# Second mixer of a hybrid decode trunk: the norm of k moved out of k and into the gates' exponent, k·k first in a head

## The reference

```python
conv = silu(causal_conv4(proj[..., :GDN_QKV]))
q = l2_normalize(conv[..., :HK]) * GDN_DK ** -0.5
k = l2_normalize(conv[..., HK:2 * HK])          # k * rsqrt(sum(k*k) + 1e-6)
v = conv[..., 2 * HK:]
g = -exp(a_log) * softplus(a + dt_bias)
beta = sigmoid(b)
# in chunks of C tokens: Gc = cumsum(g)
decay = exp(where(incl, Gc[i] - Gc[j], -inf))
M = eye(C) + where(strict, beta[i] * (k k^T) * decay, 0)
W = M^-1 (beta * exp(Gc) * k) ; U = M^-1 (beta * v)
# over the chunks: u = U - W S ; o = q_dec S + (q k^T * decay) u ; S = g_last * S + k_dec^T u
o = rms_norm(o, o_norm) * silu(z) ; y = o @ w_out
```

## Time and profile before

| what | us |
|---|---|
| median of 3 runs (lowest to highest) | 1335.26 (1334.72 to 1336.23) |
| the profiled execution, device time | 1334.86 |
| its span, first to last instruction | 1332.9 |
| TensorE busy | 1309.3 (98%) |
| VectorE / ScalarE / GpSimd busy | 634.4 / 507.1 / 365.9 |
| granted TensorE clock, mean over the span | 0.998 of full speed |

### The profile page before, as it was taken

The page is one execution under the profiler, slowest core; times in us unless marked ns, Lnnn a source line. Parts: engine busy times, 40 slices in busy tenths (PEclk is TensorE's granted clock), DMA queues, the critical chain, the costliest instruction groups (busy, mean ns, idle before and its releaser), DMA issues.

```text
span 1332.9 us, 28024 instructions
## 1 busy us (share of the span) xinstructions
PE 1309.3 (98%) x11596; PEld 1086.3 (81%) x11596; DVE 634.4 (48%) x1009; ACT 507.1 (38%) x785; POOL 365.9 (27%) x506
## 2 busy tenths in 40 slices
PE   8999999999999999999999999999999999999997
PEld 7766588888888888887778777877888888888886
DVE  5447653333333322267776677766633333332222
ACT  6243453222222322244555465545432223222221
POOL 1004324121212100165453545453221222211010
PEclk9999999999999999999999999999999999999999
DMA  8658422422232232111212221122223222233211
GB/s 264 209 191 278 143 96 95 149 102 99 94 122 104 101 121 85 63 64 40 89 41 88 88 72 57 73 96 66 96 105 116 94 94 94 94 118 131 88 44 64
DMA packets 32140, 140.89 MB, mean 106 GB/s; under 512 B 4634, under 2 KB 6938, under 8 KB 20155
## 3 DMA queue, kind: packets, MB, share of 16 engines
q1 hardware_dynamic: 32058, 139.75, 30.2%
HBM read 128.63 MB, written 11.11 MB: 105 GB/s over the span
## 4 chain that ended last, share of the span: by engine, by line
PE 92%; DVE 4%; ACT 1%; issue 1%; DMA 1%; SPq 0%; DVEq 0%; ACTq 0%
PE P L1745 64%; PE P L2110 10%; PE P L2303 2%; DVE wl L1486 1%; PE P L2288 1%; PE P L2365 1%; PE P L2296 1%; PE P L2119 1%; PE P L1823 1%; PE P L2125 1%; PE P L2331 1%; PE P L2345 1%; PE P L1955 1%; PE P L2321 1%; PE P L1898 1%
## 5 line engine op out<-in xcount | busy, mean ns | idle before, releaser
L1745 PE MATMUL P<-zh,wh 128*128 128x260 f16 x1712 | 329.2, 273 | 2.1 <-DVE wl L1194 2.1
L1745 PE MATMUL P<-zl,wh 128*128 128x260 f16 x1712 | 329.0, 273 | 0.0
L1745 PE MATMUL P<-zh,wl 128*128 128x260 f16 x1712 | 329.0, 273 | 0.0
L1174 DVE SCALAR_TENSOR_TENSOR wl<-stage,wh 128x2048 f16<-128x2048 f32 (+1 forms) x75 | 185.3, 2471 | 195.4 <-ACT wh L761 192.8
L1745 PE MATMUL P<-arena,wh 128*128 128x260 f16 x1816 | 276.2, 273 | 1.0 <-DVE hT L1391 0.3
L1745 PEld LDWEIGHTS P<-arena,wh 128*128 128x128 f16 x1816 | 175.0, 97 | 29.2 <-issue 1.3
L1745 PEld LDWEIGHTS P<-zh,wh 128*128 128x128 f16 x1712 | 164.3, 97 | 34.0 <-issue 6.7
L1745 PEld LDWEIGHTS P<-zh,wl 128*128 128x128 f16 x1712 | 165.6, 97 | 25.9
L1745 PEld LDWEIGHTS P<-zl,wh 128*128 128x128 f16 x1712 | 165.4, 97 | 25.8
L1745 PE MATMUL P<-arena,wl 128*128 128x260 f16 x908 | 174.5, 273 | 0.0
L761 ACT ACTIVATE wh<-stage 128x2048 f16<-128x2048 f32 (+1 forms) x80 | 161.8, 2023 | 3.6 <-PE P L1745 3.6
(11 more groups left out here) (366 smaller groups left out, 1646.3 us busy)
## 6 DMA issues: line engine op xcount, KB each, us to landing
stage<-w_gu SPq DMA_DIRECT2D x44, 1024.0 KB, 4.8
stage<-w_in SPq DMA_DIRECT2D x23, 1024.0 KB, 4.9
stage<-w_dn SPq DMA_DIRECT2D x16, 1408.0 KB, 5.8
arena<-cache_k SPq DMA_DIRECT2D x32, 256.0 KB, 3.5
stage<-w_out SPq DMA_DIRECT2D x8, 1024.0 KB, 5.4
arena<-cache_v SPq DMA_DIRECT2D x32, 256.0 KB, 3.0
arena<-delta_state SPq DMA_DIRECT2D x8, 512.0 KB, 3.5
o_ds<-arena SPq DMA_DIRECT2D x8, 512.0 KB, 6.8
```

The source lines that it names most:

```text
L1174: nc.vector.scalar_tensor_tensor(out=wl[:, j, 0:words], in0=stage[:, j, 0:words], scalar=WS, in1=wh[:, j, 0:words], op0=MUL, op1=SUB).then ...
L1745: mm = nc.tensor.matmul(pm[j][:, c, :], w[:, wslot, o:o + 128], x[:, k, c * CH:(c + 1) * CH], start=(k == first and w is wh and x is xh), ...
```

## The change

k stays unnormalised. With n_i = |k_i| and r_i = 1/n_i the triangular system is written in other variables (each row and column scaled by a power of the token's norm), so that beta and 1/|k|² come in as logarithms added to the exponent from which `et` is formed, and v is scaled by |k| (`kn`) instead of by beta. |k|² is the diagonal of the raw k·k.

- TensorE: k·k is the first step of a head, on raw k, and no longer needs `kb`. The 512-column broadcast of beta is gone, and `stat_l2` with it (in its place behind chunk 2 stands a `fill(1)`, taken from chunk 0, whose `fill(3)` is now `fill(2)`). The 8-column matmul over `qkp` is a 16-column one over `qkk`, moved to the head's start as the last of `gb_ps`. `k·q` waits for `rk` as well as `gd` and `bd`.
- VectorE: four `tensor_tensor_reduce` of k·k with the identity (`dg`, each two instructions) come first in a head, then `add_query` of the last head (which stood at that head's end), then `tj` (4 columns, both inputs in SBUF), then `ex` as before, `bd` as a product, no `kb`. `decode_update` has one more small step. Ahead of head 0 there are three more operations of 520 columns on 8 partitions, and beta's row is formed here.
- ScalarE: `norm_l2` is gone. Five small operations come in ahead of `et`, and `gam` moves from before `ex` to behind `yi`, ahead of the split.
- GpSimd: `square_k` and `normalize_k` are gone; `decode_products` (four small operations) moves into the previous head; `kbg` moves ahead of `om`.

The diff, cut to what the prediction speaks of (`...` marks what is left out):

```diff
@@ gpsimd, loop over the heads
-                pool.wait_ge(nq, h + 1)
-                if h >= 1:
-                    pool.wait_ge(kqs_ps, h)
-                nc.gpsimd.tensor_copy(kd2, two(k[:, SEQ:]))
...
                 pool.wait_ge(*G("gd", h + 1))
                 pool.wait_ge(st_in[h % 2], 16 * (h // 2 + 1))
...
                 nc.gpsimd.tensor_tensor(v, v, gD[:, h, :].unsqueeze(2).to_broadcast([128, NDEC, 128]), MUL
                                         ).then_inc(sdec, 1)
+                pool.wait_ge(*G("gam", h + 1))
+                if h >= 1:
+                    pool.wait_ge(*G("ws_ps", 3 * h))
+                nc.gpsimd.tensor_tensor(kbg_w, k[:, 0:SEQ], gamB, MUL).then_inc(S["kbg"], 1)
                 pool.wait_ge(*G("nf", h + 1))
...
-                pool.wait_ge(*G("gam", h + 1))
-                pool.wait_ge(*G("kk_ps", h + 1))
-                nc.gpsimd.tensor_tensor(kbg_w, kbg_w, gamB, MUL).then_inc(S["kbg"], 1)
...
-                    square_k(p)
+                    decode_products(p)
                     square_q(p)
                     decode_conv(p, (2,))
-                    normalize_k(p)
@@ scalar, loop over the heads
                 act.wait_ge(*G("gb_ps", h + 1))
-                nc.scalar.activation(gamB, P[:, 2, :], ACT.Exp).then_inc(S["gam"], 1)
                 nc.scalar.activation(gD[:, h, :], P[:, 7, 0:8], ACT.Exp).then_inc(S["gd"], 1)
+                nc.scalar.activation(rk, P[:, 7, 24:32], ACT.Ln, bias=epsc[:, 2:3]).then_inc(S["lr"], 1)
+                act.wait_ge(*G("dg", h + 1))
+                nc.scalar.activation(klog, ksq, ACT.Ln, bias=epsc[:, 2:3]).then_inc(S["lk"], 1)
+                act.wait_ge(*G("lr", h + 1))
+                nc.scalar.activation(rk, rk, ACT.Exp, scale=-0.5)
+                nc.scalar.activation(qks, P[:, 7, 16:24], ACT.Copy).then_inc(S["rk"], 1)
+                act.wait_ge(*G("lk", h + 1))
+                nc.scalar.activation(kn, klog, ACT.Exp, scale=0.5).then_inc(S["kn"], 1)
                 act.wait_ge(*G("ex", h + 1))
...
+                nc.scalar.activation(gamB, P[:, 2, :], ACT.Exp).then_inc(S["gam"], 1)
                 next_split("in1", h, 1)
...
-                                                       ACT.Copy, scale=tokm[:, c, 32 + h:33 + h])
+                                                       ACT.Copy, scale=kn[:, c:c + 1])
...
-                    if c == 2 and p < HG:
-                        norm_l2(p)
@@ vector, loop over the heads
-                dve.wait_ge(*G("gd", h + 1))
-
+                dve.wait_ge(*G("kk_ps", h + 1))
+                for c in range(4):
+                    ins = nc.vector.tensor_tensor_reduce(out=dg_out[c], in0=P[:, 6, c * 128:(c + 1) * 128], in1=ident[:, :],
+                                                         scale=1.0, scalar=0.0, op0=MUL, op1=ADD,
+                                                         accum_out=ksq[:, c:c + 1])
+                ins.then_inc(S["dg"], 1)
+                if n >= 0:
+                    add_query(n)
+                dve.wait_ge(*G("lk", h + 1))
+                link(nc.vector.tensor_tensor(tj, tokg[:, :, h], klog, ADD))
                 for c in range(4):
...
-                                                   scalar=tokm[:, c, h:h + 1], in1=msk[:, 1, :], op0=SUB, op1=MIN)
+                                                   scalar=tj[:, c:c + 1], in1=msk[:, 1, :], op0=SUB, op1=ADD)
...
-                dve.wait_ge(nq, h + 1)
-                nc.vector.tensor_tensor(kbg_w, P[:, 3, :], k, MUL).then_inc(S["kb"], 1)
+                dve.wait_ge(*G("rk", h + 1))
+                nc.vector.tensor_tensor(br, P[:, 7, 8:16], rk, MUL).then_inc(S["bd"], 1)
...
-                if p < HG:
-                    add_query(h)
@@ tensor, loop over the heads
+                pe.wait_ge(csilu, 3 * h + 2)
+                if h >= 1:
+                    pe.wait_ge(*G("u", 4 * h))
+                chunks(6, k, k, "kk_ps")
                 ready(h, "selb")
...
-                    for m, t in enumerate((g3, b3)):
-                        nc.tensor.matmul(P[:, 2 + m, :], sel3[0:72, h % 2, :], t[0:72, 0:SEQ], start=True, stop=True)
+                    nc.tensor.matmul(P[:, 2, :], sel3[0:72, h % 2, :], g3[0:72, 0:SEQ], start=True, stop=True)
                     ready(h - 1, "o")
...
-                mm.then_inc(S["gb_ps"], 1)
+                pe.wait_ge(dprep, h + 1)
+                nc.tensor.matmul(P[:, 7, 16:32], ones[:, :], qkk, start=True, stop=True).then_inc(S["gb_ps"], 1)
                 fill(4 if h < HG - 1 else 3)
...
-                chunks(6, k, kbg_w, "kk_ps")
-                ready(h, "gd", "bd")
+                ready(h, "gd", "rk", "bd")
                 chunks(7, k, q, "qk_ps")
...
-                        if c == 2:
+                        if c == 2 and h == HG - 1:
                             pe.wait_ge(snew, h + 1)
-                            if h + 1 < HG:
-                                stat_l2(h + 1)
-                            else:
-                                stat_query()
+                            stat_query()
                         else:
                             fill(1)
...
-                        fill(3)
+                        fill(2 if h < HG - 1 else 3)
```

More of the change, by code:

```diff
@@ L63 @@
 HEAD_TILES = {
-    "pe": ["gb_ps", "kk_ps", "qk_ps", "n_ps", "tk_ps"] + ["z_ps", "x_ps", "v_ps"] * 4 + ["z_ps", "tv_ps", "x_ps", "v_ps"] +
+    "pe": ["kk_ps", "gb_ps", "qk_ps", "n_ps", "tk_ps"] + ["z_ps", "x_ps", "v_ps"] * 4 + ["z_ps", "tv_ps", "x_ps", "v_ps"] +
           ["z_ps", "x_ps", "v_ps"] + ["u_ps", "ds_ps"] + ["ws_ps", "u_ps", "ds_ps"] * 3 + ["o_ps"],
-    "act": ["gam", "gd", "et", "kd4", "yi", "ye", "nf", "kd", "x"] + ["ye", "x"] * 4 + ["bv", "ye", "x"] + ["u"] * 4 + ["o"],
-    "dve": ["ex", "bd", "kb", "nt", "xt", "at"] + ["z", "xt"] * LEVELS + ["s"] + ["r", "s"] * 3,
-    "pool": ["selb"] + ["om"] * LEVELS + ["kbg", "qd"],
+    "act": ["gd", "lr", "lk", "rk", "kn", "et", "kd4", "yi", "gam",
+            "ye", "nf", "kd", "x"] + ["ye", "x"] * 4 + ["bv", "ye", "x"] + ["u"] * 4 + ["o"],
+    "dve": ["dg", "ex", "bd", "nt", "xt", "at"] + ["z", "xt"] * LEVELS + ["s"] + ["r", "s"] * 3,
+    "pool": ["selb", "kbg"] + ["om"] * LEVELS + ["qd"],
 }
@@ L201, in hybrid_trunk @@
         qq = [sq[:, 0, :], rs2[:, 0, :]]
-        gD, bD = (a2(64).rearrange("p (h b) -> p h b", h=HG) for _ in range(2))
+        tokg = rs2[:, 1, 0:32].rearrange("p (c n) -> p c n", c=4)
+        ksq, klog, kn, tj = (rs2[:, 1, 32 + 4 * i:36 + 4 * i] for i in range(4))
+        rk, br, qks = (rs2[:, 1, 48 + 8 * i:56 + 8 * i] for i in range(3))
+        gD = a2(64).rearrange("p (h b) -> p h b", h=HG)
         gate = a2(8)
@@ L222, in hybrid_trunk @@
         tailw = ddt.bitcast(f16).rearrange("p (m k n c) -> p m k n c", m=2, k=KD - EARLY_K, n=2)
+        dg_out = [t[:, i:i + 128] for t in (dt2_x, ya) for i in (256, 384)]
         bf40 = [t.bitcast(mybir.dt.bfloat16) for t in (yn1[:, 0:260], yn1[:, 260:520], ors1[:, 0:260])]
@@ L676, in _ @@
             decode_conv(0, (0, 1))
-            square_k(0)
+            decode_products(0)
             square_q(0)
@@ L2083, in _ @@
             unit("in1", 0, 1, zh, zl)
-            def stat_l2(h):
-                pe.wait_ge(nsq, h + 1)
-                for c in range(2):
-                    mm = nc.tensor.matmul(stat[:, c, :], ones[:, :], sq[:, 1, c * CH:(c + 1) * CH],
-                                          start=True, stop=True)
-                mm.then_inc(nstat, 1)
             def stat_head(h):
@@ L2143, in stat_last @@
                 mm.then_inc(o1stat, 1)
-            stat_l2(0)
             pe.wait_ge(rows_ready, 2)
             for c in range(4):
-                mm = nc.tensor.transpose(P[:, 6, 40 * c:40 * c + 40], rows[0:40, c * 128:(c + 1) * 128],
+                mm = nc.tensor.transpose(P[:, 5, 40 * c:40 * c + 40], rows[0:40, c * 128:(c + 1) * 128],
                                          ident[0:40, 0:40])
@@ L2220, in _ @@
                 if h == 0:
-                    for m in range(2):
-                        nc.tensor.matmul(P[:, 2 + m, :], selb[0:40, m, :], rows[0:40, 0:SEQ], start=True, stop=True)
+                    nc.tensor.matmul(P[:, 2, :], selb[0:40, 0, :], rows[0:40, 0:SEQ], start=True, stop=True)
                     for m in range(2):
@@ L2266, in between @@
                                              start=True, stop=True)
-                        nc.tensor.matmul(P[:, 4, 256:264], ones[:, :], qkp, start=True, stop=True)
                         nc.tensor.transpose(P[0:36, 4, 264:392], kpad[:, 0:36], ident[:, :]).then_inc(kqs_ps, 1)
```

80 lines of the change are left out of this document (34 added, 46 removed).

## The result

| | before | after |
|---|---|---|
| median, run side by side (lowest to highest), us | 1335.74 (1334.72 to 1337.71) | 1345.05 (1344.20 to 1346.29) |
| ratio, 95% interval | | 1.0070 [1.0057, 1.0083] |
| profiled execution: device time, span | 1334.86, 1332.9 | 1346.29, 1344.6 |
| granted TensorE clock, mean | 0.998 | 0.994 |

The change is slower by 0.7%: on the forecast's side, inside the range, 2.9 us above the forecast of 1342.2.

What follows compares the result with a forecast made beforehand. Up to level 0 a chain over VectorE and ScalarE paces each head, behind it TensorE's work. Heads 1 to 6 +6.5, head 7 +2.0, head 0 -1.6: +6.9 on the median 1335.26, 1342.2 us; range 1330.5 to 1346.5.

Steps and rivals of the forecast that it cites:

- The mechanism: Heads' start: `add_query` comes inside `sdec` and waits for its end; `et` 2.36 us later, `x_ps` 2.53 later.
- T0: The moment TensorE is through with a head's last step; the forecast counts each head's chain from it.
- size is no protection: Beside GpSimd even small operations are held: a 128x2 operation took 0.95 us beside a 0.95 us memset.
- Heads 1 to 6: Each +1.08 us: 2.53 later at `x_ps`, less 0.88 for `stat_l2` and 0.57 in the levels; +6.5 together.
- level waits of rows 3: Two recurring TensorE waits, 0.24 + 0.34 us a head, in level 1; all 0.57 a head taken as gained.
- Head 7: Last head, with no `stat_l2` behind it: +2.0 us.
- Head 0: No `add_query`; `sdec` starts earlier, giving 0.7 of L1589's 0.89 us block, plus 0.88 for `stat_l2`: -1.6 us.
- TensorE's waits: Idle about 0.8 us before `k·q`, 1.5 or more before level 0's `z_ps`, and before `x_ps`; 3 a head together.
- Rival 1: `add_query` is not held up by `sdec`; `x_ps` only 0.98 us later, -4.0 in all, 1331.3 us; 18%.
- Rival 3: `add_query` gets there first and `tj` waits 1.9 us for `sdec`; +2.9 us, 1345 us; 15%.
- Rival 2: TensorE's work paces after all, ScalarE's chain having hidden slack; -11.2 us, 1324 us; 6%.
- Rival 4: Partial hold or half a us of chain slack; it all but cancels, result within 0.2%; 14%.

Runs made afterwards that it cites:

- experiment 2: The change with `add_query` moved behind `bd`, so that `tj` meets `sdec`; 1338.76 us, ratio 1.0026.
- Experiment 1: The change with GpSimd's `sdec` made to wait for `ex` as well; 1333.2 us, ratio 0.9975 to the kernel before.
- experiment 3: The change with `add_query` behind `bd` and the logarithm that `tj` adds put in PSUM (`tj` also waits for `kn`); 1331.06 us, ratio 0.9972.
- experiment 5: The change with two fp32 matmuls of `stat_l2`'s size put back behind chunk 2 of heads 0 to 6; 1357.54 us, ratio 1.0165.
- experiment 6: The change with 28 small fp16 matmuls filling TensorE's idle time before `z_ps`; 1344.50 us, ratio 1.0061.
- experiment 4: The change with `gam` moved ahead of `et`, `kbg` waiting for `yi` and `ex` for `gam`; 1341.63 us, ratio 1.0045.
- 7: The change unaltered again, 1343.53 us; and the change with 28 small matmuls before `z_ps` and 12 before level 0's `x_ps`, 1342.94 us.
- 10: `gam` moved ahead of `et` in two kernels: that of experiment 3, 1333.45 us, and that of Experiment 1, 1333.08 us.
- 8: The kernel of Experiment 1 with 8 small matmuls before `z_ps` and 12 before level 0's `x_ps`; 1330.58 us, ratio 0.9957.
- 9: The kernel of 8 with head 0's `kbg` waiting for the second `xt`; 1329.86 us, ratio 0.9959.

## Why the prediction was right, and where it was not

**The mechanism was the forecast's.** Each step of the chain, counted from T0:

| step | forecast | measured |
|---|---|---|
| `dg` starts | 1.17 | 1.09 |
| `sdec` starts | 1.88 | 1.83 |
| `add_query` ends | 4.34 | 4.29 |
| `ex` starts | 4.48 | 4.39 |
| `et` starts | 5.70 | 5.62 |
| `x_ps` starts | 14.00 | 13.81 |

It rested on rows 10 and 11, an operation of another line and size beside GpSimd, and the estimate that `add_query` ends 0.56 behind `sdec` was exact. Rows 12 and 13, which the text took for "size is no protection", are another case (one SBUF input, beside a memset that reads none); that the width doesn't help is shown by `tj` in experiment 2. Experiment 1 shows the cause by taking it away, and experiment 3 by taking away one SBUF input alone.

**Heads 1 to 6**: +0.92 each against +1.08. `x_ps` is 2.34 later instead of 2.53, since from `et` to `x_ps` only 0.06 came in and not 0.48 - 0.31 = 0.17 (from `ye`'s start to `nf`'s it was 0.74 before and is 0.32, so 0.42 went and not 0.31; the rest is the 0.08 by which `et` is earlier). From `x_ps` to the next T0 a head took 32.40 us and takes 30.98: of the 1.42, `stat_l2` is 0.88 (experiment 5), and 0.54 is left for the level waits of rows 3, where 0.57 was taken. 2.34 - 1.42 = 0.92. **Head 7**, with what follows it: +2.2 against +2.0.

**Head 0 failed**: -0.25 against -1.6. The step was "`sdec` starts earlier now". It started at 597.13 (596.91 before), so the first `xt` was still held. `normalize_k` is gone from ahead of it, but GpSimd begins its work for head 0 later, at 590.26 and not at 588.01: it waits for ScalarE's silu of q and k (L993), which starts at 589.04 and not at 586.77, behind the rows of the gates, in which VectorE has more to do now. The text counted this extra work for TensorE's start alone (which is 590.71 in both kernels), and not for GpSimd's. And the text has `kbg` run beside L1589 in every head, with time to spare in `ye`, without asking what that does in head 0, where `kbg` follows `sdec` at once, holds the second `xt` too (1.38 instead of 0.43), and `ye` has nothing to spare. Of the changed kernel, VectorE and then GpSimd, head 0:

```profile
597.47 1.84 DVE L1595 TENSOR_TENSOR arena<-arena 128x256 f32<-128x256 f32 x1
599.34 1.38 DVE L1596 TENSOR_TENSOR arena<-arena,ident 128x256 f32<-128x256 f32 x1
```

```profile
590.26 0.19 POOL L643 COPY arena<-arena 128x8 f32<-128x8 f32 x1 [9.19 <-ACT arena L993]
...
597.13 1.90 POOL L701 TENSOR_TENSOR arena<-arena 128x1024 f32<-128x1024 f32 x1 [0.24 <-POOL arena L623]
598.98 1.45 POOL L706 TENSOR_TENSOR arena<-arena 128x512 f32<-128x512 f32 x1
```

`x_ps` of head 0 came at 604.26, 1.15 later than the 603.11 of before, where I had it 0.7 earlier.

**TensorE's waits**: 0.66 before `x_ps` was called, and before `z_ps` it was 1.41 where 1.5 or more was. Before k·q it was 0.26 and not 0.8: `stat_head`, which stands ahead of k·q, waits 0.20 for `add_query` first, and TensorE's work up to there took some 0.3 more than the text has. The waits are 2.53 us a head together, not 3. That `add_query`, moved into the next head, has a reader there was not in the text.

**The clock was not in the sum.** Without its falls in the heads the change takes 1342.1 us (1346.29 - 4.24 = 1342.05; the profiled execution of experiment 6, 1342.12). The forecast of 1342.2 is that number, partly by luck: head 0 was 1.3 too low, heads 1 to 6 were 1.0 too high, head 7 0.2 too low, 0.4 lay in putting the sum on the median, and the part of the device time that lies outside the span was 0.25 shorter. The falls are the term that the prediction put at nothing: it foresaw 3 us a head of idle time and gave it its own length as price. The profile shows them as 4.24 us; what the median has above 1342.1, 2.9 us in one set and 1.4 in the other, is of their size, but the other executions have no profile. The evidence that idle time brings them on is good and not complete. In five profiles of kernels with the full idle time (the change twice, experiments 4, 5 and 2, the last with less before `z_ps` and more before `stat_head`) four have a fall in the heads; experiment 4, with 0.93 us before `z_ps`, is the one without. In the two profiles of the change with the filling (experiments 6 and 7) there is none. The four kernels of experiments 1, 3 and 10, with mostly 0.5 us or less before `z_ps`, have none either, so that the two filled kernels built on number 1 (8 and 9) add nothing by their profiles, but their executions have lost the upper group. Which head is hit differs from execution to execution, and what decides that stays open. The Trainium skill ("TensorE: Matmul & The Clock Gate", Part 1) has the clock follow how busy TensorE has been; that fits these rows.

**The rivals.** Rival 1 priced the chain without the hold at 1331.3 us; experiment 1, which makes it so, gave 1333.2 in the median and 1329.53 in its profiled execution, which has no fall in the heads. Rival 3 described what experiment 2 built: `tj` held by `sdec`. It took 0.6 us a head less than the forecast's case, not 0.41 more, because `add_query` then no longer stands ahead of `ex`, and because `tj` was ready 0.57 us into `sdec` and not at its start. Rival 2 is ruled out up to `x_ps` by the waits; behind `x_ps`, experiment 5 shows that TensorE's work does set the pace. Rival 4, a result within 0.2%, is outside the interval, 1.0057 to 1.0083.

## What to carry to other kernels

When a step is moved to another place in one engine's order, ask what GpSimd runs at that moment: in these runs a VectorE operation with two inputs in SBUF, 4 columns wide or 520, ended only behind the GpSimd operation that was there first, and the price falls on all that is queued behind it. Before giving up a change for this, try the cheap ways out: let the GpSimd operation wait until the chain has passed, or put one of the inputs into PSUM. Each moves the hold or the slack elsewhere, so two such gains don't simply add (experiment 10). And where the new idle time of a busy TensorE comes in gaps close together, its price can be more than its length; read the granted clock in short windows behind the gaps, and compare kernels by their undisturbed periods.

## What the runs showed of the hardware

- An operation of 4 columns with both inputs in SBUF took 1.35 us beside `sdec`, what was left of it, and 0.16 us in the middle of it with one input in PSUM (experiments 2 and 3).
- The GpSimd side was longer too, though less: `sdec` took 2.09 us instead of 1.90 where it started beside VectorE's convolution (experiment 1). What in the convolution makes it so was not told apart.
- In a kernel whose TensorE is busy 97% of the time, idle gaps of 1.41 and 0.66 us, with 1.2 us of work between them, were followed in some heads by several us at 1.2 GHz, 2.87 and 1.37 us longer in the profiled execution. With small matmuls of no use in these gaps, the two profiles of the change showed no fall in the heads, and the period stayed at 44.79.
